# A hybrid decoder trunk on one NeuronCore: mLSTM sums with tokens on the partitions, and a spread-out modulation

## What is computed

```python
# mlstm_group: 4 heads of 128, 2 chunks of 128 tokens (t: query token, s: key token, e: channel)
Sw = einsum('bhctd,bhcsd->bhcts', qc, kc) * exp(Dlog - m_t[..., None])
num = einsum('bhcts,bhcse->bhcte', Sw, vc) + inter[..., None] * einsum('bhctd,bhcde->bhcte', qc, C_prev)
den = sum(Sw, axis=-1) + inter * einsum('bhctd,bhcd->bhct', qc, n_prev)
h = num / maximum(abs(den), exp(-m_t))[..., None]
h = sigmoid(o_pre) * rmsnorm(h, norm_g)
# trunk, per layer
mod = (silu(c) @ w_ada[l] + b_ada[l]).reshape(B, 6, D)
x = x + gt1 * rmsnorm(hybrid_mixer(h) , g_post_mix[l])      # the mixer ends in y @ w_out
h = rmsnorm(x, g_pre_ffn[l]) * (1.0 + sc2) + sh2
```

## Time and profile before

| what | us |
|---|---|
| median of 3 runs (lowest, highest) | 2665.36 (2662.74, 2665.84) |
| the profiled execution | 2654.51 |
| its span in the trace | 2652.7 |
| PE busy / weight loads | 2433.4 (92%) / 2138.5 (81%) |
| DVE busy | 2013.8 (76%) |
| ACT busy | 1289.0 (49%) |
| POOL busy | 292.5 (11%) |
| mean granted PE clock (share of 2.4 GHz) | 0.972 |
| DMA, mean over the span | 242 GB/s |

### The profile page before, as it was taken

How to read it: one execution, slowest core, us unless ns; L and a number is a source line. 1 busy time by engine, 2 the same in 40 slices (tenths; PEclk the granted TensorE clock), 3 DMA queues, 4 the chain that set the end, 5 groups by cost and what they waited for, 6 DMA issues and landing times.

```text
span 2652.7 us, 41129 instructions
## 1 busy us (share of the span) xinstructions
PE 2433.4 (92%) x14388; PEld 2138.5 (81%) x14388; DVE 2013.8 (76%) x2444; ACT 1289.0 (49%) x2025; POOL 292.5 (11%) x434
## 2 busy tenths in 40 slices
PE   1599989977999999999998999998899999999998
PEld 1499878855888888878888999886688888887886
DVE  8897988778989999966667978766688666665555
ACT  1365456434544444444447545654544555554444
POOL 1031321102111111101000322000010000000000
PEclk9999899988999999999999999999999999999999
DMA  9657877557798989868775677554388555555564
GB/s 396 265 195 260 303 257 248 204 206 274 264 338 326 335 333 330 311 228 276 266 267 174 226 275 247 169 204 151 127 287 300 188 189 188 188 190 174 192 194 152
DMA packets 193004, 643.13 MB, mean 242 GB/s; under 512 B 28480, under 2 KB 38736, under 8 KB 190960
## 3 DMA queue, kind: packets, MB, share of 16 engines
q1 hardware_dynamic: 125056, 455.96, 48.8%
q0 software_dynamic: 47216, 170.80, 18.5%
q10 hardware_dynamic: 20608, 14.72, 1.8%
HBM read 626.68 MB, written 14.71 MB: 242 GB/s over the span
## 4 chain that ended last, share of the span: by engine, by line
PE 69%; DVE 20%; DMA 4%; issue 3%; ACT 3%; POOL 0%; DVEq 0%; ACTq 0%; POOLq 0%; SPq 0%
PE ps L1116 21%; PE ps L658 17%; PE ps L1117 10%; PE ps L643 8%; DVE ada_acc L1607 6%; DVE w_lo L1601 4%; PE ps L980 4%; DVE mix L1601 3%; DMA ada_w<-ada_d 2%; ACT w_hi L1178 1%; DMA ring<-stream 1%; PE ps L601 1%; PE ps L628 1%; DVE mix L1607 1%; PE ps L775 1%
## 5 line engine op out<-in xcount | busy, mean ns | idle before, releaser
L1601 DVE TENSOR_TENSOR w_lo<-ring,w_hi 128x1024 fp32r<-128x1024 f32 x744 | 918.0, 1238 | 523.9 <-ACT w_hi L1178 522.5
L1178 ACT ACTIVATE w_hi<-ring 128x1024 fp32r<-128x1024 f32 x744 | 786.6, 1058 | 920.0 <-PE ps L1117 327.5
L1116 PE MATMUL ps<-hT,w_hi 128*128 128x512 f32 x2688 | 937.6, 395 | 4.0 <-DVE w_lo L1601 4.0
L1117 PE MATMUL ps<-hT,w_lo 128*128 128x256 f32 x2688 | 747.2, 278 | 0.0
L1116 PEld LDWEIGHTS ps<-hT,w_hi 128*128 128x128 f32 x2688 | 504.2, 188 | 124.1 <-DVE w_lo L1601 4.9
L1117 PEld LDWEIGHTS ps<-hT,w_lo 128*128 128x128 f32 x2688 | 505.7, 188 | 0.0
L643 PE MATMUL ps<-hT,w_hi 128*128 128x256 f32 x2496 | 473.2, 292 | 10.0 <-DVE w_lo L1601 9.3
L1607 DVE SCALAR_TENSOR_TENSOR ada_acc<-ada_w,cs,ada_acc 128x1024 f32<-128x1024 f32 x348 | 445.9, 1282 | 22.2 <-DMA ada_w<-ada_d 8.6
L643 PEld LDWEIGHTS ps<-hT,w_hi 128*128 128x128 f32 x2496 | 400.4, 197 | 16.1 <-issue 15.0
L643 PE MATMUL ps<-hT,w_lo 128*128 128x256 f32 x1248 | 358.7, 287 | 0.0
L643 PEld LDWEIGHTS ps<-hT,w_lo 128*128 128x128 f32 x1248 | 245.3, 197 | 0.0
(11 more groups left out here) (262 smaller groups left out, 2494.6 us busy)
## 6 DMA issues: line engine op xcount, KB each, us to landing
ring<-stream SPq DMA_DIRECT2D x760, 512.0 KB, 4.4
ada_w<-ada_d POOLq DMA_DIRECT2D x320, 512.0 KB, 5.6
ring<-ada_d SPq DMA_DIRECT2D x36, 512.0 KB, 9.9
ada_w<-ada_d SPq DMA_DIRECT2D x28, 512.0 KB, 10.0
xs<-x SPq DMA_DIRECT2D x2, 2048.0 KB, 10.1
s_in_w<-mix ACTq DMA_DIRECT2D x8, 512.0 KB, 3.6
s_out_w<-mix ACTq DMA_DIRECT2D x16, 256.0 KB, 5.7
ring<-s_in_w SPq DMA_DIRECT2D x8, 512.0 KB, 5.7
```

Of the source, the lines that this page charges most:

```text
L1116: pe.matmul(ps[:, bank, :], w_hi[:, s, ks], hT[:, k, :, :], start=k == 0, stop=False)
L1117: m = pe.matmul(ps[:, bank, SEQ:2 * SEQ], w_lo[:, s, ks], hT_hi[:, k, :], start=False, stop=k == KT - 1)
L1178: s.activation(w_hi[:, c % SPLIT, :], ring[:, at % RING, :], ACT.Copy).then_inc(hi_ready, 1)
L1601: return v.tensor_tensor(o, a, b, op)
```

## The change

The mLSTM's sums are turned round, so that tokens are on the partitions:

- PE: `m_sums` takes the weights of the tokens as the stationary operand. Numerators are [token, channel]; a divisor is one column, a product with one column of ones (128x1). The state's normaliser `n` is one column per head, too. The floors `exp(-m_t)` reach the partitions by two small transposes at input tile 35 into a larger `bcol`; both floor selections in the projection go. `m_back` (L1019 of the changed kernel) transposes four heads of the finished, normed numerators back.
- ACT: no `m_absolute`, no `m_square`. `m_root` is four 128x128 Squares that read the numerators in PSUM, scale them by the inverse divisor and sum along the free axis, then a Sqrt of 128x4.
- DVE: `m_inverse` (three operations of 128x4), `m_normed` (two of 128x4 and one product of 128x512 with a broadcast column), `m_gated` (the gate and the gain, from PSUM). The four 128x512 reciprocals per layer go.
- The steps stand at other pieces, all before piece 6; `m_root(1)` stands before ACT's piece 4, `m_back(1)` before PE's piece 5.
- The modulation of layer 0's projection: one chunk behind each of the pieces 0 to 27, two behind 28 and 29.

```diff
                 def m_sums(ck, num, den):
                     for h in range(MH):
-                        pe.matmul(ps[:, num, hs], vm[:, ck, h, :], m_swb[ck][:, hs], start=True, stop=ck == 0)
-                        if ck:
-                            pe.matmul(ps[:, num, hs], m_C[:, hs], m_qib[:, hs], start=False, stop=True)
-                        m = pe.matmul(ps[:, den, hs], ones, m_swb[ck][:, hs], start=True, stop=ck == 0)
-                        if ck:
-                            m = pe.matmul(ps[:, den, hs], m_n[:, hs], m_qib[:, hs], start=False, stop=True)
+                        pe.matmul(ps[:, num, hs], m_swb[ck][:, hs], vm[:, ck, h, :], start=True, stop=ck == 0)
+                        m = pe.matmul(ps[:, den, col], m_swb[ck][:, hs], ones[:, 0:1], start=True, stop=ck == 0)
+                        if ck:
+                            pe.matmul(ps[:, num, hs], m_qib[:, hs], m_C[:, hs], start=False, stop=True)
+                            m = pe.matmul(ps[:, den, col], m_qib[:, hs], m_n[:, h:h + 1], start=False, stop=True)
...
+                def m_back(ck, bank):
+                    m_h.wait(pe, l, ck + 1)
+                    for h in range(MH):
+                        m = pe.transpose(ps[:, bank, h * P:(h + 1) * P], m_hb[:, h * P:(h + 1) * P], ident)
+                    m_tr.by(m)
...
                 def m_root(ck, bank):
+                    m_inv.wait(s, l, ck + 1)
+                    for h in range(MH):
+                        m = s.activation(m_tb[:, hs], ps[:, bank, hs], ACT.Square, scale=m_r[ck][:, h:h + 1],
+                                         accum_out=m_ssq[ck][:, h:h + 1])
+                    m_ss.by(m)
                     m_ss.wait(s, l, ck + 1)
-                    m_rs.by(s.activation(m_e2, ps[:, bank, :], ACT.Sqrt, bias=K("eps"), scale=1.0 / HD))
+                    m_rs.by(s.activation(m_q[ck], m_ssq[ck], ACT.Sqrt, bias=K("eps"), scale=1.0 / HD))
...
+                def m_inverse(ck, den):
+                    m_num.wait(v, l, ck + 1)
+                    step(stt(m_q[ck], d, -1.0, bcol[:, 2 + ck, :], ALU.mult, ALU.max))
+                    step(tt(m_q[ck], m_q[ck], d, ALU.max))
+                    m_inv.by(v.reciprocal(m_r[ck], m_q[ck]))
...
                 piece(0)
+                m_inverse(0, 6)
+                out_ada(1)
                 piece(1)
-                m_heads(0, 3, 6)
-                piece(2)
+                m_normed(0, 3)
                 m_qi.wait(v, l, 1)
...
                 m_weights(1, 7)
+                out_ada(1)
+                piece(2)
+                m_gated(0, 3)
+                out_ada(1)
                 piece(3)
+                m_inverse(1, 7)
+                out_ada(1)
                 piece(4)
-                m_normed(0)
-                m_heads(1, 6, 2)
+                m_normed(1, 6)
+                out_ada(1)
                 piece(5)
-                piece(6)
-                piece(7)
-                m_normed(1)
-                for j in range(8, 2 * KT - 2):
+                m_gated(1, 2)
+                out_ada(1)
+                for j in range(6, 2 * KT - 2):
...
                     piece(j)
-                    if j >= KT - 2:
-                        out_ada(2)
+                    out_ada(1 if j + AHEAD < 2 * KT else 2)
...
-                out_ada(2 * UCH)
```

More of the change, by code:

```diff
@@ L399, in trunk @@
         m_hb, m_tb = m_buf(0), m_buf(1)
-        m_e1, m_e2 = m_buf(2), m_buf(3)
+        m_ssq, m_r, m_q, m_f = ([att_s[:, ck, 4 * i:4 * i + 4] for ck in range(2)] for i in range(4))
+        M_DEN = 16
         def head_slot(n):
@@ L948, in _ @@
                         for ck in range(2):
-                            m = pe.transpose(ps[:, 7, 4 * ck:4 * ck + 4], rows(3, ck * P, (ck + 1) * P), K("ident", 0, 4, 4))
+                            pe.transpose(ps[:, 7, 4 * ck:4 * ck + 4], rows(3, ck * P, (ck + 1) * P), K("ident", 0, 4, 4))
+                        m_row.wait(pe, l, 1)
+                        for ck in range(2):
+                            m = pe.transpose(ps[:, 7, 8 + 4 * ck:12 + 4 * ck], rows(0, ck * P, (ck + 1) * P), K("ident", 0, 4, 4))
                         mb_mm.by(m)
@@ L1042, in _ @@
                     pe.matmul(ps[:, 7, hs], m_kwb[:, hs], vm[:, 0, h, :], start=True, stop=True)
-                    m = pe.matmul(ps[:, 2, hs], m_kwb[:, hs], ones, start=True, stop=True)
+                    m = pe.matmul(ps[:, 2, h:h + 1], m_kwb[:, hs], ones[:, 0:1], start=True, stop=True)
                 m_c.by(m)
                 piece(1)
-                m_abs.wait(pe, l, 1)
-                select(6, 0, 0)
-                m_floor.by(m_last[0])
-                piece(2)
                 m_cev.wait(pe, l, 2)
@@ L1055, in _ @@
                 m_qi.by(m_last[0])
-                piece(3)
-                m_squares(0, 3)
-                piece(4)
-                m_h.wait(pe, l, 1)
+                piece(2)
+                m_back(0, 3)
                 m_sw.wait(pe, l, 2)
@@ L1064, in _ @@
                 m_sums(1, 6, 7)
-                select(2, 0, 1)
-                m_floor.by(m_last[0])
-                piece(5)
-                piece(6)
-                m_abs.wait(pe, l, 2)
-                m_squares(1, 7)
-                for j in range(7, KT):
+                piece(3)
+                piece(4)
+                m_back(1, 2)
+                for j in range(5, KT):
                     piece(j)
-                m_rs.wait(pe, l, 2)
+                m_out.wait(pe, l, 2)
                 for j in range(KT, 2 * KT - 2):
@@ L1503, in _ @@
                 piece(0)
-                m_absolute(0, 6)
                 m_c.wait(s, l, 1)
                 m_cev.by(s.activation(m_C, ps[:, 7, :], ACT.Copy))
-                m_cev.by(s.activation(m_n, ps[:, 2, :], ACT.Copy))
+                m_cev.by(s.activation(m_n[:, 0:MH], ps[:, 2, 0:MH], ACT.Copy))
+                m_root(0, 3)
                 piece(1)
@@ L1511, in _ @@
                 piece(2)
-                m_square(0)
                 piece(3)
-                m_root(0, 3)
+                m_root(1, 6)
                 piece(4)
-                m_absolute(1, 7)
-                piece(5)
-                m_square(1)
-                piece(6)
-                m_root(1, 7)
                 glu_y.wait(s, l, 1)
-                for j in range(7, 2 * KT - 2):
+                for j in range(5, 2 * KT - 2):
                     if j == KT - 4:
```

45 lines of the change are left out of this document (18 added, 27 removed).

## The result

| | before | after |
|---|---|---|
| median of the runs (lowest, highest) | 2658.42 us (2652.92, 2665.84), 6 runs | 2632.51 us (2627.05, 2641.49), 6 runs |
| ratio, 95% interval | | 0.9905 (0.9886 to 0.9923) |
| the profiled execution, its span | 2654.51, 2652.7 | 2627.05, 2625.2 |
| layer 0: piece 0 to 16, 16 to the norm | 71.8, 68.3 | 68.8, 47.5 |
| layer 1: piece 0 to 16, 16 to the norm | 71.7, 46.0 | 67.9, 45.9 |

The forecast was 2641 us within 2633 to 2652, a gain of 24.0. The ratio is a gain of 25.3 us (20.5 to 30.3). The gain is what can be compared. The profiled execution of the changed kernel is the fastest of its six.

What follows compares the result with a forecast made beforehand. The prediction took layer 0's second half of the output projection to be bound by DVE and DMA in turn. Layer 0's -21.5 and layer 1's -2.5 us made -24.0, from 2665.4 to 2641 us, range 2633 to 2652.

Steps and rivals of the forecast that it cites:

- The bound: Output projections: DVE and DMA bound layer 0's second half in turn; two modulation chunks behind each piece cost 22.4 us.
- The first half: Piece 0 to piece 16 of each layer's output projection: old stalls go, a new one comes, -2.5 us per layer.
- The stall: New PE wait at `m_back(1)`, ahead of piece 5, in each layer: 7.5 us.
- its half clock: PE running slowly behind the new wait ahead of piece 5: 2.5 us per layer.
- The chain: Work from the end of PE's piece 3 to `m_back(1)`, crossing twice between ACT and DVE: 10.5 us.
- The second half of layer 0: Piece 16 to the norm: -22.4 us by spreading the modulation, +1.5 for gated halves, +1.0 for the reload.
- The gated halves: Two 128x1024 operations after piece 17, 2.5 us on DVE, meet no slack in layer 0: 1.5 us come back.
- the reload of `xs`: SP's 2.1 MB load now falls among layer 0's modulation chunks: 1 us added, bounds 0 and 4.
- DMA is full: Rival, chance 0.15: loads limit layer 0's second half; reload costs 4 us, late chunks 2 more: 2645 to 2648 us.
- The milder and the worse stall: Rivals on the wait before piece 5: milder, chance 0.12, 2633 us; worse, chance 0.10, 2647 us.
- The spread gives nothing: Rival, chance 0.03: layer 0's second half was bound by loads and stays so; only first halves count, 2660 us.
- Slower than before: Rival, chance 0.02: PE stays at half clock through pieces 5 to 15 after the long wait: 2696 us.

Runs made afterwards that it cites:

- e11: Changed kernel with the modulation scheduled as in the kernel before, leaving the mLSTM part alone; repeat run: ratio 0.9974 (0.9957 to 0.9991) to the kernel before.
- e2: Kernel before with only the modulation spread, one chunk behind each piece: ratio 0.9956 (0.9933 to 0.9979) to the kernel before.
- e9: Changed kernel with 7 unread filler products on PE between piece 4 and the second transposes back: ratio 0.9876 (0.9853 to 0.9899).
- e5: Changed kernel with 14 unread filler products on PE between piece 4 and the second transposes back: ratio 0.9927 (0.9904 to 0.9949).
- e3: Changed kernel with the second transposes back ahead of PE's piece 7 and their gated product behind DVE's piece 7: ratio 0.9894 (0.9847 to 0.9940).
- e10: Changed kernel with only the second root moved on ACT, behind piece 4 instead of ahead of it: ratio 0.9882 (0.9862 to 0.9902).
- e6: Changed kernel with activations split before weights, second root behind ACT's piece 4, second transposes ahead of piece 7 and gated product behind it: 2611.06 us, ratio 0.9825.
- e7: Kernel of e6 with the two gated halves taken apart by one piece on ACT and DVE: median 2604.82 us, ratio 0.9797 (0.9770 to 0.9825).

## Why the prediction was right

By its own steps, against the stages of the profiled execution:

- **The bound.** That two chunks behind each piece made layer 0's second half 22 us longer than layer 1's is shown from both sides: with the old schedule it stays at 68.3 us (e11), with the spread alone it falls to 49.0 (e2). It was DVE's work for the most part (61.1 us) and its waits for chunks that came late (6.3).
- **The first half**, forecast at -2.5 in layer 1 and, with the chunks, -1.6 in layer 0: measured -3.8 and -3.0. The stall was forecast at 7.5 and is 7.27; its half clock at 2.5 and is 2.1 (e9); the chunks in layer 0 at 0.9 and are 0.9. One term was mis-sized: a sum of squares was put at 0.46, as "2 of a piece's 12 passes". Its operands are plain fp32, and such a product takes 0.87 (e5). So 1.7 us went and not 0.9, while the half clock behind the first old stall was smaller by 0.4. The transposes take 0.41 each at the full clock (535.19 - 534.78 in e9) and not 0.6, and the waits ahead of `m_sums(1)` are 0.27 and not 0.7. These small terms, 0.4 each and all on one side, are 1.2 of the 1.3 us per layer. The stall (0.2) and its half clock (0.4) go the same way; against them, piece 0 with the sums of chunk 0 took 8.0 and 8.1 us from its start to piece 1's, 7.8 and 7.7 before, where the forecast had no change. All this is within what the clock alone does: the first half of the code of before took 70.3 us in layer 1 of e2, so that the same change would read as -2.4.
- **The chain.** Its path was right: e3 and e10 each moved one link, e6 both, and the wait became as short as the chain says (3.15, 5.66, 0.21). Its length was forecast at 10.5 us from the end of piece 3; piece 4 (2.85) and the wait (7.27) make 10.1.
- **The second half of layer 0**, forecast at -22.4 + 1.5 + 1.0 = -19.9: measured -20.8. Which side of the forecast it fell on is luck: e2, e3, e9 and e10 have the same stage there and took 49.0 to 49.1 us at a clock of 0.97, which would be -19.3. The gated halves cost 1.2 us more than in layer 1 (2.17 against 0.98 in the second of the two waits); 1.5 had been said. The 1.0 for the reload of `xs` was not to be seen: it landed in 11.5 us, and DVE waited for a chunk for 0.1 us in the whole window (and for 0.99 at the last chunk, behind it, of which 0.4 reached the norm).
- **The loads.** The forecast took 370 GB/s for the most that this stage allows, from 359 at a share of 0.97, and weighed 396 against it. The stage did 402 at a full share. The 358 GB/s that the Trainium skill (DMA: Bandwidth & Descriptors, section "Where 436 GB/s comes from") gives as a core's limit on the HBM side was exceeded over such a stretch here, where one core ran alone; no run shows what a core gets with others at work. The rival "DMA is full" falls for the change; with the moves of e7 its share is 1.00, and DVE still waited for only 0.4 us (and 0.9 at the last chunk).
- **The other rivals.** The milder and the worse stall: 7.27 us and 2.1 decide against both. "The spread gives nothing": 14.7 us in e2. "Slower than before": behind the stall the transposes and two thirds of piece 5 at half clock, then the full one. Two sums in the rivals don't come out. The price of "DMA is full", 3 for the reload and 2 for late chunks, gives 2644 to 2646 and not 2645 to 2648. And 12 us more per layer, with the 2.5 already counted, are 14.5 / 2.8, some 5 pieces at half clock and not 9. Neither moves the forecast or its range.
- **The sum**, -24.0, against -27.8 in the profiled execution and 25.3 (20.5 to 30.3) by the ratio. The 3.8 us between the sums are 2.7 in the two first halves and 0.9 in layer 0's second half, with rounding; the ratio can't tell the two sums apart. So the mechanism and the size of the large terms are shown, and that the total came within some 1 to 4 us is in part luck.

## What to carry to other kernels

Where an engine's work in a loop has slack in each turn, spread the extra work over all turns, one piece per turn; but first clear the long operations out of the turns that you want to use, since a part whose own gain is small (here 4 us per layer) can decide what the other part is worth (15 us or 18 to 20). When a stall is replaced by another, follow the chain through the queues and look for the work that merely stands behind it: four moves of a line or two each, with nothing computed otherwise, were worth another 28 us (e7). And split first what is needed first: operands that are four turns ahead can wait, those of the turn after next can't.
